# A hybrid retention and expert layer: one expert pair loaded ahead of the sort, the last gate gathers later, the third residual on GpSimd, the tail's return products reordered

## The reference

```python
hid = silu(einsum('td,edf->tef', t, we_g)) * einsum('td,edf->tef', t, we_u)
routed = einsum('tef,efd->td', hid * combine[..., None], we_d)
shared = (silu(t @ ws_g) * (t @ ws_u)) @ ws_d
x = x + g2 * (routed + shared)          # g2: one row for context, one for latent tokens
y = rmsnorm(x, final_norm_g)
```

## Time and profile before

| | |
|---|---|
| median of 3 runs (lowest, highest) | 895.19 us (893.06, 895.57) |
| the profiled execution's own time | 895.6 us |
| its span | 893.8 us, granted clock 0.995 |
| PE, DVE, ACT, POOL busy | 97%, 53%, 19%, 7% |
| DMA | 288 MB, busy 90% or more of every slice from about 360 to 850 us |

### The profile page before, as it was taken

One profiled execution on the slowest core, in us unless ns is written; L12 is line 12 of the kernel. 1 busy time (PEld: TensorE's weight loads), 2 busy tenths in 40 slices (PEclk: granted clock), 3 DMA queues, 4 the chain that ended last, 5 costly groups with the idle time before them and its releaser, 6 DMA issues.

```text
span 893.8 us, 11385 instructions
## 1 busy us (share of the span) xinstructions
PE 868.0 (97%) x4186; PEld 445.6 (50%) x4186; DVE 472.6 (53%) x1031; ACT 166.7 (19%) x349; POOL 58.3 (7%) x75
## 2 busy tenths in 40 slices
PE   7999999999999999999999999999999999999884
PEld 6774446777655547644544444434444444444332
DVE  3645398936796945434443444435444353535447
ACT  4131012020000034121111112112121212111113
POOL 1020100000000000100000000000000000000000
PEclk9999999999999999999999999999999999999998
DMA  9998433512575847499999999999999999999981
GB/s 330 389 368 226 148 125 126 197 50 92 224 279 201 352 192 259 162 408 419 421 418 419 417 419 417 418 418 409 412 421 418 421 418 421 418 420 418 418 328 74
DMA packets 63626, 288.00 MB, mean 322 GB/s; under 512 B 6472, under 2 KB 6528, under 8 KB 38480
## 3 DMA queue, kind: packets, MB, share of 16 engines
q1 hardware_dynamic: 56176, 265.60, 74.8%
q0 software_dynamic: 7392, 21.63, 6.5%
HBM read 287.34 MB, written 4.33 MB: 326 GB/s over the span
## 4 chain that ended last, share of the span: by engine, by line
PE 89%; DMA 8%; DVE 2%; SPq 1%; issue 1%; ACT 0%; DVEq 0%
PE bank L1270 23%; PE bank L834 12%; PE bank L1295 11%; PE bank L827 9%; PE bank L1313 9%; DMA ring<-in_w_exp_up 6%; PE bank L1051 5%; DMA ring<-in_w_ada 2%; PE bank L1212 2%; PE bank L1098 1%; PE bank L1215 1%; PE bank L839 1%; PE bank L844 1%; PE bank L1311 1%; PE bank L1004 1%; PE bank L1006 1%
## 5 line engine op out<-in xcount | busy, mean ns | idle before, releaser
L1270 PE MATMUL bank<-ring,QK 128*64 128x512 f32 (+1 forms) x1056 | 228.3, 602 | 5.8 <-DMA ring<-in_w_exp_up 5.8
L2286 DVE TENSOR_TENSOR hT<-bank,hT 128x512 f32<-128x512 f32 x174 | 109.7, 684 | 83.1 <-PE bank L1313 82.2
L1270 PEld LDWEIGHTS bank<-ring,QK 128*64 128x64 f32 (+1 forms) x1056 | 71.4, 130 | 128.3 <-issue 128.3
L2275 DVE SCALAR_TENSOR_TENSOR VG<-VG,cw,bank 128x256 f32<-128x256 f32 x32 | 15.4, 480 | 170.9 <-issue 164.9
L1295 PE MATMUL bank<-ring,VG 128*64 128x512 f32 (+1 forms) x512 | 102.2, 598 | 0.4 <-ACT VG L1656 0.4
L834 PE MATMUL bank<-hT,ring 128*128 128x384 f32 x256 | 86.0, 489 | 0.0
L827 PE MATMUL bank<-ring,hT 128*128 128x512 f32 x192 | 82.7, 593 | 0.0
L1313 PE MATMUL bank<-y_hi,slotT 128*128 128x512 f32 x180 | 80.9, 449 | 0.0
L1313 PE MATMUL bank<-y_lo,slotT 128*128 128x512 f32 x180 | 70.9, 394 | 0.0
L1663 ACT CAST y_hi<-bank 128x512 fp32r<-128x512 f32 x60 | 32.3, 589 | 195.2 <-PE bank L1313 191.9
L834 PEld LDWEIGHTS bank<-hT,ring 128*128 128x128 f32 x256 | 47.8, 190 | 33.7 <-issue 2.4
(11 more groups left out here) (425 smaller groups left out, 950.4 us busy)
## 6 DMA issues: line engine op xcount, KB each, us to landing
ring<-in_w_exp_gate SPq DMA_DIRECT2D x56, 1024.0 KB, 12.3
ring<-in_w_exp_up SPq DMA_DIRECT2D x56, 1024.0 KB, 15.1
ring<-in_w_exp_down SPq DMA_DIRECT2D x56, 1024.0 KB, 17.0
ring<-in_w_ada SPq DMA_DIRECT2D x12, 2048.0 KB, 12.2
ring<-in_w_in SPq DMA_DIRECT2D x9, 2048.0 KB, 18.0
spare<-in_w_exp_gate SPq DMA_DIRECT2D x8, 1024.0 KB, 11.2
spare<-in_w_exp_up SPq DMA_DIRECT2D x8, 1024.0 KB, 14.4
spare<-in_w_exp_down SPq DMA_DIRECT2D x8, 1024.0 KB, 18.7
```

Source lines behind the costliest of these rows:

```text
L1270: ins = mm(ps[0][rows, :], xT[:, k, rows], gate_up_of(p, n)[:, k, :, :], start=(k == 0), stop=(k == KC - 1))
L2286: v.tensor_tensor(into, o, into, ALU.add).then_inc(sem("summed"), 1)
```

## The change

1. `AHEAD` has six experts: pair 2's (8 and 9) are fixed too. SP no longer waits for `order_ready` before pair 2 but before pair 3; the first of pair 2's loads (into `spare`) waits for `h2_written` instead.
2. The gate gather of pair 30 waits for one gate_up more (31 instead of 30), that of pair 31 for the load `g2_rows_in` (the broadcast rows of g2 that SP issues at pair 31) instead of `gate_up_done`.
3. `residual(2)` moves from DVE to GpSimd.
4. TensorE: the first three of pair 30's return tiles stand before hidden_T(31). Pair 31's return products go by halves: three high parts, then three low parts. DVE forms pair 31's remainder of the first half before it gates the second.
5. The last tile is normed and stored in two halves.

```diff
-AHEAD = (4, 5, 6, 7)
+AHEAD = (4, 5, 6, 7, 8, 9)
...
-            sp.wait_ge(sem("order_ready"), 1)
             for p in range(2, PAIRS):
-                e = [sp.value_load(column(tab_order, 2 * p + n), min_val=0, max_val=E - 1) for n in range(2)]
+                if p == 3:
+                    sp.wait_ge(sem("order_ready"), 1)
+                if 2 * p < len(AHEAD):
+                    e = AHEAD[2 * p:2 * p + 2]
+                else:
+                    e = [sp.value_load(column(tab_order, 2 * p + n), min_val=0, max_val=E - 1) for n in range(2)]
                 for n in range(2):
                     if p == 2 and n == 0:
                         sp.wait_ge(sem("x0_parked"), 16)
-                        computed(sp, "h2T01")
+                        sp.wait_ge(sem("h2_written"), 16 * TT)
...
             def gather_gates(p):
-                pool.wait_ge(sem("gate_up_done"), p)
-                pool.wait_ge(sem("scattered"), 72)
+                if p == LAST - 2:
+                    pool.wait_ge(sem("gate_up_done"), p + 1)
+                else:
+                    pool.wait_ge(sem("g2_rows_in"), 16)
+                pool.wait_ge(sem("scattered"), 6 * (SHARED_FROM + 12))
...
                 if p in slot_gate:
                     gather_gates(p)
+            pool.wait_ge(sem("g2_rows_in"), 16)
+            pool.wait_ge(sem("summed"), 6 * (LAST - 2))
+            sum_2 = hTf[:, 2 * D:3 * D]
+            nc.gpsimd.tensor_tensor(sum_2, sum_2, g2_rows[:, 1, :], ALU.mult).then_inc(sem("pool_formed"), 1)
+            pool.wait_ge(sem("pool_formed"), 1)
+            nc.gpsimd.tensor_tensor(x[:, 2, :], x[:, 2, :], sum_2, ALU.add).then_inc(sem("pool_formed"), 1)
...
+            def scatter_last():
+                p = LAST - 1
+                for h in range(2):
+                    tiles = range(3 * h, 3 * h + 3)
+                    pe.wait_ge(sem("hi_ready"), 2 * p + h + 1)
+                    for n in tiles:
+                        return_part(p, n, y_hi, False, False)
+                    pe.wait_ge(sem("lo_ready"), 2 * p + h + 1)
+                    for n in tiles:
+                        return_part(p, n, y_lo, False, True).then_inc(sem("scattered"), 1)
...
             gate_up(LAST - 1)
+            scatter_next_to_last(range(3))
             hidden_T(LAST - 1)
-            scatter_two(LAST - 2)
+            scatter_next_to_last(range(3, 6))
             down(LAST - 1)
-            scatter_two(LAST - 1)
+            scatter_last()
...
                 if last:
                     residual(1)
-                    residual(2)
...
-                v.scalar_tensor_tensor(x[:, t, :], x[:, t, :], rstd[:, t:t + 1], fin_g, ALU.mult, ALU.mult).then_inc(sem("out_ready"), 1)
+                for cut in out_cuts[t]:
+                    v.scalar_tensor_tensor(x[:, t, cut], x[:, t, cut], rstd[:, t:t + 1], fin_g[:, cut], ALU.mult, ALU.mult).then_inc(sem("out_ready"), 1)
```

More of the change, by code:

```diff
@@ L392, in trunk_kernel @@
         slot_gate = {LAST - 2: AB1[:, 0:1024], LAST - 1: Fm[:, 2048:3072]}
+        out_cuts = [[slice(0, D)], [slice(0, D)], [slice(0, 512), slice(512, D)]]
         base_3 = small[:, 304:307]
@@ L635, in _ @@
             further_rounds(sp, load_next, load_first)
[L636 to L640, removed]
+            for n, (t, cut) in enumerate((t, cut) for t in range(TT) for cut in out_cuts[t]):
+                sp.wait_ge(sem("out_ready"), n + 1)
+                dst = y_prompt[0, :, cut] if t == 0 else y_sample[0, (t - 1) * P:t * P, cut]
+                sp.dma_start(dst, x[:, t, cut]).then_inc(sem("out_written"), 16)
+            sp.wait_ge(sem("out_written"), 16 * sum(len(cuts) for cuts in out_cuts))
         def gather(pool, n, k, landed):
@@ L1372, in scatter, with return_part, scatter_next_to_last @@
                     scatter_tile(p, g, FREE_FIRST)
-            def scatter_two(p):
-                first = p == LAST - 2
-                if first:
+            def return_part(p, n, y, start, stop):
+                t, h = LAST_TILES[n]
+                return mm(ps[LAST_BANKS[n]][:, :], slotT[p % KEEP][:, t * P:(t + 1) * P], y[:, h * 512:(h + 1) * 512], start=start, stop=stop)
+            def scatter_next_to_last(tiles):
+                p = LAST - 2
+                if 0 in tiles:
                     pe.wait_ge(sem("summed"), 6 * p)
[L1378 to L1381, removed]
+                    pe.wait_ge(sem("lo_ready"), 2 * p + 2)
+                for n in tiles:
+                    if LAST_BANKS[n] == 1:
                         pe.wait_ge(sem("hidT_ready"), LAST)
[L1383 to L1386, removed]
+                    return_part(p, n, y_hi, True, False)
+                    return_part(p, n, y_lo, False, False).then_inc(sem("scattered"), 1)
+            def scatter_last():
[6 more added lines that the diff above has]
+                    pe.wait_ge(sem("lo_ready"), 2 * p + h + 1)
+                    for n in tiles:
+                        return_part(p, n, y_lo, False, True).then_inc(sem("scattered"), 1)
             slots_of(2)
@@ L2296, in remainder_gated, with gated @@
                 dve.wait_ge(sem("gates_in"), 16 * (j + 1))
-                for h in range(2):
+                def gated(h):
                     cut = slice(h * 512, (h + 1) * 512)
@@ L2302, in remainder_gated, with low @@
                     v.tensor_tensor(y_gated[h], ps[2 + h][:, :], slot_gate[p][:, cut], ALU.mult).then_inc(sem("y_gated"), 1)
-                for h in range(2):
+                def low(h):
                     cut = slice(h * 512, (h + 1) * 512)
@@ L2306, in remainder_gated @@
                     v.tensor_tensor(y_lo[:, cut], y_gated[h], y_hi[:, cut], ALU.subtract).then_inc(sem("lo_ready"), 1)
+                gated(0)
+                if j:
+                    low(0)
+                gated(1)
+                if not j:
+                    low(0)
+                low(1)
             def pair_weights(p):
@@ L2348, in residual @@
                 else:
-                    dve.wait_ge(sem("x_formed"), t)
+                    dve.wait_ge(sem("x_formed"), 2 * t)
                 tile_sum = hTf[:, t * D:(t + 1) * D]
-                v.tensor_tensor(tile_sum, tile_sum, gate[t], ALU.mult).then_inc(sem("sum_gated"), 1)
-                dve.wait_ge(sem("sum_gated"), t + 1)
+                v.tensor_tensor(tile_sum, tile_sum, gate[t], ALU.mult).then_inc(sem("x_formed"), 1)
+                dve.wait_ge(sem("x_formed"), 2 * t + 1)
                 v.tensor_tensor(x[:, t, :], x[:, t, :], tile_sum, ALU.add).then_inc(sem("x_formed"), 1)
@@ L2392, in last_sums @@
             def last_sums(low, high):
-                dve.wait_ge(sem("x_formed"), TT)
+                dve.wait_ge(sem("x_formed"), 2 * (TT - 1))
                 for n, (t, h) in enumerate(LAST_TILES):
@@ L2397, in last_sums @@
                     dve.wait_ge(sem("scattered"), 6 * (LAST - 1) + n + 1)
+                    if n == 2:
+                        dve.wait_ge(sem("pool_formed"), 2)
                     if n == 5 and low == "x2_low":
@@ L2430, in rounds_to_x @@
                     tile_sum = hTf[:, t * D:(t + 1) * D]
-                    v.tensor_tensor(tile_sum, tile_sum, gate[t], ALU.mult).then_inc(sem("sum_gated"), 1)
-                    dve.wait_ge(sem("sum_gated"), TT + t + 1)
+                    v.tensor_tensor(tile_sum, tile_sum, gate[t], ALU.mult).then_inc(sem("x_formed"), 1)
+                    dve.wait_ge(sem("x_formed"), 2 * (TT - 1) + t + 1)
                     v.tensor_tensor(x[:, t, :], x[:, t, :], tile_sum, ALU.add).then_inc(sem("x2_ready"), 1)
```

## The result

The changed kernel takes 909.51 us (median of 6 runs, 909.07 to 913.13), the kernel before on the same chip 894.89: a ratio of 1.0175, 95% interval 1.016 to 1.019, or +14.6 us where +8.1 was forecast. The profiled execution took 909.6 us with a span of 907.7 (before 895.6 and 893.8), at a mean granted clock of 0.987 (0.995). PE's busy time grew by 3.6 us (871.6 against 868.0) in a span 13.9 us longer, so most of the loss has to be looked for in waits.

A forecast was written before the change was run, and what follows sets the result against it. Bound by TensorE's own work and, in the last pairs, the DMA backlog. Terms 9.7 - 1.1 - 0.5 = +8.1 on the profiled 895.6 gave 903.7, median 903.3 us; range 899.5 to 905.5, with the obstruction 906.5.

The forecast's parts named there:

- the largest term: Pair 30's later gate gather holds back pair 31's token gather in GpSimd's queue, so TensorE stands: +9.7 us.
- Pair 2 ahead of the sort: Start, weight loads: earlier loads only fill idle DMA time, as SP's next load waits for gate_up(0): 0, bound +1.
- The gate gather of pair 30: GpSimd's queue: pair 31's tokens land at 864.9, TensorE stands 13.9 us, gate_up(31) ends at 881.9: +9.7 us.
- the two ends given: Landing of pair 31's tokens: 864.9 if the two gathers go in a row, 863.1 if they overlap fully.
- The gate gather of pair 31: GpSimd's queue near the end: the gate rows still arrive before DVE needs them near 886.8: 0 us.
- The return tiles: TensorE ahead of hidden_T(31): three tiles cover 1.16 us of waiting, down(31) 3.1 us behind gate_up(31): -1.1 us.
- The third residual: residual(2) moved to GpSimd near the end: wholly hidden, 0 us, with 0 to +2.5.
- the other mechanism: Rival, 18 in 100: GpSimd and DVE obstruct each other; hidden activations late by up to 2.9 us, 906.2.
- the 1.5 to spare: DVE's queue has 1.5 us to spare before it must form pair 31's hidden activations.
- The bound of +2.5: Upper bound for the third residual: DVE's own instructions give way for two GpSimd instructions of 2.0 us.
- Halves: Pair 31's last products and remainder by halves, at the end: 0 us, bounds -1.2 and +0.3.
- Last store: Span's end: storing the last tile in halves saves half of 512 KB at 0.41 MB/us, less 0.1: -0.5 us.

The follow-up runs named there:

- the first experiment: Kernel before with only pair 2's experts fixed and its first two loads held by h2_written: 896.92 us against 893.46, ratio 1.0032.
- the last version: Kernel before plus return tiles, late gate gathers behind pair 31's token gather, early load behind the first gather, last store in halves: 892.48 us, ratio 0.9981.

## Why the prediction was wrong where it was

The direction, the mechanism of the largest term and most of the size came as forecast. Two terms of the sum were mis-sized, and they make up 4.7 of the 5.9 us between 903.7 and the profiled 909.6.

**Pair 2 ahead of the sort: forecast 0 with at most +1, measured +3.5 alone (2.9 by the ratio).** This is the step that failed. It priced the early load against the first gather only, with 5 us for the two megabytes from a start "well before 364"; they took 7.3 us and landed at 367.8. More than that, the gather reads two stores, the token rows and the weights, and the early load waits for the first and goes ahead of the second. GpSimd's timeline of before showed that store at 360.40 and its landing in 2.2 us; both would have warned. In the changed kernel the delay is 4.0 us at SP's next load and 3.1 us at gate_up(30), which starts at 847.13 where 844.0 was forecast.

**The gate gather of pair 30: right in its mechanism, and closer in its sum than in its parts.** From gate_up(30)'s start to gate_up(31)'s end the forecast had 37.9 us, and it was 37.7. That closeness is partly luck, since two misses of 0.8 and 0.6 us cancel. Inside: the tokens landed 12.1 us after GpSimd issued the gate gather (forecast 12.9), the stall was 13.1 us (13.9), and the work behind it took 10.5 (9.9), since the low clock cost 2.3 us and not 1.7. The gathers overlapped in part, between the two ends given: landings of 8.6 and 10.8 us instead of one after the other. The experiment with this part alone gives the absolute times within 0.5 us.

**The gate gather of pair 31: 0, right.** In the changed kernel no wait for the gate rows shows; the gather left at 869.58 and VectorE used it at 891.66.

**The return tiles: −1.1, right alone, absent in the changed kernel.** There down(31) started 4.7 us behind gate_up(31), not 3.1. The tiles ran in the gap (884.80 to 886.5), but TensorE then waited 1.41 us for hidden activations.

**The third residual: forecast 0, in fact what ate the tiles' gain.** Here the other mechanism, which had 18 in 100, came on top of the forecast. The two remainders lost 1.1 and 2.2 us while GpSimd worked, 3.3 in all; less the 1.5 to spare that leaves 1.8, and 1.6 was seen at down(31). Against keeping the residual on VectorE the net price was 0.8 by the profile of the experiment that puts it back, where VectorE's extra work let the sums start 0.7 us later behind down(31). The bound of +2.5 held; the value taken was the wrong end. The Trainium skill's page "SBUF — State Buffer", section "SBUF: two separate sides", names the pair that excludes each other, a VectorE instruction with two SBUF inputs and a GpSimd one that reads SBUF. The traces agree: y_lo, which reads QK or AB and y_hi, was stretched until 0.54 us behind each GpSimd instruction, and was not with GpSimd idle (0.69 us each with the residual back on VectorE); the gating with an input in PSUM was not stretched (0.68 us).

**Halves: 0 with +0.3 at most, measured +0.3 in the trace. Last store: −0.5, measured 0.** The time behind the last norm is nearly all fixed, and I had priced it by the megabyte. A further 0.4 us stands before the first norm in the changed kernel. It shows in the profiles of all eight kernels with six fixed experts and in none of the six with four. So it comes with the first part of the change, and with the 3.1 us at the start it makes 3.5, which agrees with what this part costs alone. Why it comes is open.

The sum, from the profile: 3.1 (start) + 1.6 (hidden activations) + 0.3 (halves) + 0.5 (store) + 0.4 (open) = 5.9, as 909.6 − 903.7 is; the 0.2 us by which the middle was shorter than forecast, and roundings, are left out. The range up to 906.5 had room for one of the two misses, not for both.

## What to carry to other kernels

Before a load is moved earlier, list every transfer that the next step waits for, small stores too, and see which of them it now overtakes. An early load whose buffer's successor is tied to compute won nothing here, so it can be put behind all of these for free. When a wait in an in-order queue is made later, what stands behind it must be put ahead first; and work that is moved to an idle engine isn't free for a busy one whose instructions it holds up. Last, before two kernels are compared by one profile each, see at which clock each of them ran behind its waits.

## What the runs showed of the chip

- A 96 KB store of GpSimd's queue landed in 2.2 us on idle DMA engines and in 6.8 (7.1 in the first experiment) behind two 1 MB loads of SP issued up to 0.6 us before it: about the time the second of these took itself (7.3 us). Here the small transfer paid for its neighbours, not for its size.
- VectorE's instructions beside GpSimd's 128x1024 additions and products (2.39 to 2.70 us each): 0.69 became 1.81 and 2.85, 0.28 became 2.40, 1.22 became 2.23.
- The granted clock fell to its lower level behind waits of 2.3 and 2.5 us at the start (gate_up(0) took 8.47 and 9.40 us instead of 7.09) and behind 2.60 and 2.62 us ahead of gate_up(31) (8.77 us). It did not behind 2.33 us there in the kernel with the tiles alone, nor behind 2.81 us in the last version (7.07 us each, the clock at 1.00 throughout). So a wait for weights can cost 1.7 us beyond its own length, the length alone doesn't say whether it will, and kernels with the same waits can differ by it.
